# Layer 0 decode attention: cached value pages loaded as 32 partitions of 8 KB in place of 128 partitions of 2 KB

## The reference, cut to what matters

```python
k_past = gather_pages(past['cache_fox_k'][e], page_table)
v_past = gather_pages(past['cache_fox_v'][e], page_table)
...
logits = jnp.einsum('bqhd,bkhd->bhqk', qi, k) * scale
logits = logits + ci[..., :, None] - cum[:, :, None, :]
p = masked_softmax(logits, mask)
return jnp.einsum('bhqk,bkhd->bqhd', p, v)
```

## Time and profile before

| | us |
|---|---|
| median of 3 runs | 2722.32 |
| lowest, highest | 2717.17, 2731.27 |
| the profiled execution | 2733.98 |
| its span | 2732.3 |
| the stage, from the first value transfer to the last write of H | 376.5 to 575.2 |

### The profile page before, as it was taken

How to read it: one execution, slowest core, us unless ns; L and a number is a source line. 1 busy time by engine, 2 the same in 40 slices (tenths; PEclk the granted TensorE clock), 3 DMA queues, 4 the chain that set the end, 5 groups by cost and what they waited for, 6 DMA issues and landing times. The chain is left out here.

```text
span 2732.3 us, 46037 instructions
## 1 busy us (share of the span) xinstructions
PE 2242.2 (82%) x16993; PEld 1947.3 (71%) x16993; DVE 1200.7 (44%) x2134; ACT 582.1 (21%) x999; POOL 270.1 (10%) x433
## 2 busy tenths in 40 slices
PE   3994447776999999697569997999996676999898
PEld 2862443354999999694369885778884356999898
DVE  3313721124544442534455655556453345444433
ACT  2101121101111000301135454445331112101000
POOL 0010223310000000000012212112101300000000
PEclk8996678888999999898679898999997988999999
DMA  6551059963232231222300005333235831332321
GB/s 258 195 219 43 5 182 386 386 261 116 73 90 84 83 107 44 70 86 97 142 1 2 1 2 154 93 93 118 68 93 193 312 109 39 93 91 86 96 91 55
DMA packets 238575, 321.92 MB, mean 118 GB/s; under 512 B 17851, under 2 KB 196104, under 8 KB 230959
## 3 DMA queue, kind: packets, MB, share of 16 engines
q1 hardware_dynamic: 211671, 199.44, 22.5%
q0 software_dynamic: 26720, 120.09, 12.0%
HBM read 311.56 MB, written 16.42 MB: 120 GB/s over the span
## 5 line engine op out<-in xcount | busy, mean ns | idle before, releaser
L381 PE MATMUL ps<-XHup,WHup 128*128 128x272 f32 x1408 | 294.3, 291 | 28.8 <-DVE XLup L357 25.3
L381 PE MATMUL ps<-XLup,WHup 128*128 128x272 f32 x1408 | 292.7, 289 | 0.0
L381 PE MATMUL ps<-XHup,WLup 128*128 128x272 f32 x1408 | 291.5, 288 | 0.0
L381 PEld LDWEIGHTS ps<-XHup,WHup 128*128 128x128 f32 x1408 | 222.8, 190 | 30.8 <-DVE XLup L357 26.8
L1954 PE MATMUL ps<-CHi,W1H 128*128 128x512 f32 (+1 forms) x512 | 207.2, 405 | 19.9 <-DVE CLo L2023 19.9
L381 PEld LDWEIGHTS ps<-XLup,WHup 128*128 128x128 f32 x1408 | 223.5, 190 | 0.0
L381 PEld LDWEIGHTS ps<-XHup,WLup 128*128 128x128 f32 x1408 | 222.1, 190 | 0.0
L2023 DVE TENSOR_TENSOR CLo<-RAWc,CHi 128x512 fp32r<-128x512 f32 x128 | 139.9, 1115 | 163.1 <-ACT CHi L1977 163.1
L1955 PE MATMUL ps<-CLo,W1H 128*128 128x512 f32 (+1 forms) x512 | 205.3, 401 | 0.0
L1956 PE MATMUL ps<-CHi,W1L 128*128 128x512 f32 (+1 forms) x512 | 204.6, 400 | 0.0
L1977 ACT CAST CHi<-RAWc 128x512 fp32r<-128x512 f32 x128 | 143.2, 1151 | 155.4 <-PE ps L1956 135.1
(11 more groups left out here) (458 smaller groups left out, 4135.5 us busy)
## 6 DMA issues: line engine op xcount, KB each, us to landing
RAWup<-in_w_up SPq DMA_DIRECT2D x88, 512.0 KB, 3.9
Wmod<-in_w_mod POOLq DMA_DIRECT2D x20, 2048.0 KB, 10.6
VP<-in_cache_fox_v POOLq DMA_DIRECT2D x128, 256.0 KB, 6.1
KP<-in_cache_fox_k SPq DMA_DIRECT2D x128, 256.0 KB, 11.3
RAWdn<-in_w_down SPq DMA_DIRECT2D x14, 1408.0 KB, 6.4
RAWin<-in_nsa_w_in SPq DMA_DIRECT2D x20, 512.0 KB, 3.6
KS<-in_cache_nsa_ks SPq DMA_DIRECT2D x80, 128.0 KB, 2.8
Wmod<-in_w_mod SPq DMA_DIRECT2D x4, 2048.0 KB, 19.2
```

Of the source, the lines that this page charges most:

```text
L381: mm = self.nc.tensor.matmul(self.ps[:, banks + n, 0:HALF], w, x[:, n * HALF:(n + 1) * HALF], start=start, stop=stop)
```

## The change

The load puts four adjoining tokens of a page, 8 KB that are contiguous in HBM, on one partition. So a page takes 32 partitions: page n of a sequence goes to the partitions 32*(n % 4) to 32*(n % 4)+31, and the four pages of a quarter lie below each other in one column range of VP, 8 KB wide. Weighted sums take the tokens 4c+n of every page in matmul n, so each of the four turns takes every fourth column of PR. The numbers of transfers, matmuls and turns stay, and so do VP's size, the two slots, and all waits.

```diff
-        v_pages = i["cache_fox_v"][0].rearrange("n t h d -> n t (h d)")
+        v_pages = i["cache_fox_v"][0].rearrange("n (c x) h d -> n c (x h d)", x=PER)
...
-            KP, VP = sb("KP", [P, 2, PAGES, 512]), sb("VP", [P, 2, PAGES, 512])
+            KP, VP = sb("KP", [P, 2, PAGES, 512]), sb("VP", [P, 2, QUARTERS, PER * 512])
...
-                            pool.dma_start(VP[:, b % 2, n, :], v_pages[ds(page, 1), :, :].rearrange("a p f -> p (a f)")).then_inc(v_full[b % 2], 16)
+                            pool.dma_start(VP[32 * (n % PER):32 * (n % PER) + 32, b % 2, n // PER, :], v_pages[ds(page, 1), :, :].rearrange("a c f -> c (a f)")).then_inc(v_full[b % 2], 16)
...
-                            nc.tensor.transpose(ps[:, TURN, n * P:(n + 1) * P], PR[:, n * P:(n + 1) * P], self.ident)
+                            nc.tensor.transpose(ps[:, TURN, n * P:(n + 1) * P], PR[:, :].rearrange("r (c x) -> r x c", x=PER)[:, n, :], self.ident)
...
-                                                 VP[:, s, PER * a + n, :], start=(n == 0), stop=(n == PER - 1 and a > 0), skip_group_check=True)
+                                                 VP[:, s, a, n * 512:(n + 1) * 512], start=(n == 0), stop=(n == PER - 1 and a > 0), skip_group_check=True)
```

## The result

| | before | after |
|---|---|---|
| median of 6 runs each, us | 2725.4 | 2820.7 |
| span of the profiled execution, us | 2732.3 | 2820.0 |
| stage: from SEL's issue to the last write of H, us | 375.0 to 575.2, 200.2 | 374.6 to 669.6, 295.0 |

The changed kernel is slower: ratio 1.0342, with a 95% interval from 1.032 to 1.0364, about 95 us. The stage alone grew by 94.8 us, so all of it lies there. The two spans differ by 88 only, as the profiled execution of before had a longer remainder: runs of one kernel spread over 14 us.

What follows compares the result with a forecast made beforehand. The prediction took the DMA engines as the bound, with PE's own chain second. Slower landing less larger packets' saving gave +60 us, turns hidden and issue nothing: 2782 us on the median of 2722.3, range 2713 to 2802.

Steps and rivals of the forecast that it cites:

- The bound: In the stage's loads: DMA engines limit, PE's chain is 1.6 us a sequence below, and every microsecond of delay reaches the total.
- Part 1, larger packets: Value loads in 8 KB rows: 81.1 us of engine time, a term of -7.9 us if landing costs nothing.
- Part 2, the landing: Value pages landing on 32 partitions instead of 128: +50 to +73 us, taken as +60, larger packets' saving included.
- the middle case: Landing of value pages: two engines share one door, 16 engines reach the rate of 8, 0.634 us per 8 KB packet.
- the sum over the cycle: Value and key queues taking turns by packet: 256 cycles plus remaining keys make 231 or 254 us, against 181 now.
- Where it would show: PE's waits for keys: start +20 to +25 us later, the other 35 to 40 us in later sequences' waits.
- Part 3, turns: L1453's 32 weight loads taking every fourth column: +2.3 us at most, hidden where PE waits longer for keys.
- Part 4, issue: POOL's DMA instruction for 32 rows: about 400 ns, pitch from 1.15 to 1.0 us, nothing while values are backlogged.
- Free landing: Rival on page landing: 32 partitions accept as fast as 128, or at 1.13 the cost; 2716 or 2725 us, chance 0.28.
- the quarter rate: Rival on page landing: 32 of 128 partitions give a quarter of the rate, +235 us, chance 0.04.
- the cutting into 2 KB: Rival on value rows: 8 KB is cut into 2 KB pieces again, larger packets' gain is gone, 2790 us; no chance given.
- the sooner keys: Rival on key loads: first keys come 3.3 us earlier and all 10.9 us of later waits go; 2708 us, chance 0.06.

Runs made afterwards that it cites:

- the gather: Changed kernel, but one indirect transfer brings four pages of the same 8 KB rows to all 128 partitions: 2728.5 us, ratio 1.0003 to the kernel before.
- the pair of runs on 0 to 63 and 32 to 95: Changed kernel with 4 KB rows and half the value pages, all landing on partitions 0 to 63 or on 32 to 95: 2718.0 and 2718.6 us.
- The run with keys first: Changed kernel with one more wait on POOL, so a sequence's values are issued only when its keys have landed: 2804.1 us, ratio 1.0276.

## Why the prediction was right in kind and wrong in size

**The bound.** Right. The DMA engines bound the stage and nobody had slack: 93.9 us of new waits for keys are 94.8 us of stage and 95 us of total.

**Part 1, larger packets.** Right in its term: 81.1 us of engine time for values, which the gather shows within 1 us. What it would have brought was too high even where landing is free. I let DMA's 7.9 us shrink the waits, and overlooked that the faster values also delay the first keys, by 6.5 us.

**Part 2, the landing.** That landing decides is shown by the pair of runs on 0 to 63 and 32 to 95. The choice of the middle case over the short burst of the earlier trace rows was right. "Two engines share one door", so that a packet takes twice as long, is near but not shown: 0.572 against 0.320 us is a factor of 1.8.

The step that failed is the sum over the cycle, "+50 to +73, of which I take +60". It let a key packet cost nothing while values hold the doors, or 0.090 us where it doesn't fit. Measured in 470 to 493 it is 0.150, while a value packet there took 75.6% x 23 x 16 / 3.92 x 0.008192 = 0.581 and not 0.634. Over the stage the terms came out as follows. Values: the cycle had 162 us, measured 145.5, 16 less. Keys: +60 means 241 us for both queues, which leaves 79 for keys; measured 119.2, or 117 without the 2 us of other transfers on q1, 38 more. The sum of both queues is 264.7 against 183.2, +81.5, above my upper end of +73. Why the keys pay that much stays open: a key page goes to all 128 partitions, so doors alone would slow the half of its packets that wants the values' doors, but in 480 to 520 of the trace hardly one key packet in a hundred took under 110 ns, where before nearly all did.

**Where it would show.** I expected the first wait at 53 to 58 us; it is 59.6. The later waits I spread evenly, "some 10 us for each that finds a backlog". They came as two of 37 and 38 us, with nearly free sequences between them. This rhythm carries the stage from +81.5 to +94.8. The transfers end at about 640.5 where it was about 555.2, 85 us later; the 4 us beyond +81.5 lie in stretches such as 442 to 450, where the engines' share is 0.71 to 0.77. Behind the last transfer PE had one sequence left, 20.0 us; now it has one and a half, 29.1 us, while the DMA engines stand idle. I hadn't priced these 13 us: my sum ended where engine time ends. The run with keys first bears on it, 16.6 us less with the same landing.

**Part 3, turns.** Right: 212 ns for 140, 2.3 us, hidden by waits.

**Part 4, issue.** Wrong in size, without an effect that a run shows: 492 ns for 32 rows where I had 400, and a page every 1.14 us, not 1.0. My 1.15 for the kernel before doesn't follow from the rows I named, which give (68.7 + 145.3) / 128 = 1.67 with the slot waits; it is the pitch between them, as from 377.69 to 395 in POOL's timeline.

**The rivals.** Free landing fell, and so did the quarter rate, the cutting into 2 KB (6144 packets on q0, two fifths fewer than the 10232 of the earlier trace rows) and the sooner keys; the 3.3 us of the last should have been 28 x (1 - 81.1 / 89.0) = 2.5. The missing 35 us are thus the keys' own slow-down (38 us above what I had), less what values took below my price (16), and 13 us of rhythm that engine time doesn't show.

## What to carry to other kernels

In these runs a transfer's rate depended on which partitions it landed on more than on how many: before packing rows to make packets longer, see that each single transfer still reaches both halves, 0 to 63 and 64 to 127. Where two queues share the engines, a slow landing in one makes the other slow as well, so price both, and then follow the order in which the consumer needs them up to the end of the last chain; engine time alone is a lower bound. A saving on a stream that waits for nothing else moves the bound to the next engine, here PE's own 20.4 us a sequence.

## What I had not expected of the hardware

A 2 KB packet of keys to all partitions rose from 90 to 150 ns while another queue was landing on one half; with the other queue's 8 KB packets on all partitions it stayed at 90. One queue of 256 KB pages from SP fills the engines to 0.77 and 233 GB/s. And a transfer to the partitions 32 to 95 is as fast as one to all 128 (0.174 us for 4 KB), while 0 to 63 takes 0.265.
